# A two-layer attention kernel in a rebuilt form: weights split a unit ahead, norm and shared keys and values merged into the output of layer 0, plain f32 in layer 1's attention

## The reference, cut to what matters

```python
# layer 0: differential attention, 8 heads of two sub-heads of 64, causal with ALiBi
u = rms_norm(h, g) * (1 + scale) + shift
q, k, v, z = split(u @ w_in)                 # q and k normed per 64
o = (softmax(q1 k1) - lam * softmax(q2 k2)) @ v
h = h + gate * ((rms_norm(o, g2) * 0.8 * silu(z)) @ w_out)
# shared keys and values, made once from h
ks, vs = split((rms_norm(h, gkv) * (1 + s) + t) @ w_kv)   # ks normed; 2 heads of 64
# layer 1: 16 heads of 64 in two groups, window of 128 keys, a learned sink per head
u = rms_norm(h, gb) * (1 + scale) + shift
q, z = split(u @ w_in)                       # q normed per 64
o = softmax_with_sink(q ks) @ vs             # each 128 queries see 256 keys
h = h + gate * ((o * silu(z)) @ w_out)
```

## Time and profile before

| | us |
|---|---|
| median of 3 runs | 1358.45 |
| profiled execution | 1358.09 |
| its span | 1356.3 |
| busy PE / PEld / DVE / ACT / POOL | 1174.1 / 928.2 / 856.5 / 700.0 / 232.9 |
| mean granted clock of PE, of full speed | 0.967 |

### The profile page before, as it was taken

The page is one execution under the profiler, slowest core; times in us unless marked ns, Lnnn a source line. Parts: engine busy times, 40 slices in busy tenths (PEclk is TensorE's granted clock), DMA queues, the critical chain, the costliest instruction groups (busy, mean ns, idle before and its releaser), DMA issues.

```text
span 1356.3 us, 22457 instructions
## 1 busy us (share of the span) xinstructions
PE 1174.1 (87%) x6192; PEld 928.2 (68%) x6192; DVE 856.5 (63%) x2676; ACT 700.0 (52%) x2161; POOL 232.9 (17%) x354
## 2 busy tenths in 40 slices
PE   0469899998989899998975997679999898985998
PEld 0457576676757676675754885568888787875886
DVE  6665766666676766667664324976887888776221
ACT  0655555555555556555554104966776776674100
POOL 1201212112121211212101221111211212110122
PEclk9989999999999999999997998879999999997999
DMA  8342131312222131222214334110020100113332
GB/s 296 118 139 65 50 101 42 111 55 87 71 72 85 57 101 42 89 71 69 86 39 144 122 126 171 63 63 5 13 75 17 58 31 24 62 32 112 116 122 85
DMA packets 53226, 111.42 MB, mean 82 GB/s; under 512 B 5904, under 2 KB 19216, under 8 KB 52112
## 3 DMA queue, kind: packets, MB, share of 16 engines
q1 hardware_dynamic: 53136, 110.51, 24.8%
HBM read 93.71 MB, written 16.78 MB: 81 GB/s over the span
## 4 chain that ended last, share of the span: by engine, by line
PE 69%; DVE 12%; issue 8%; ACT 6%; DMA 3%; POOL 1%; DVEq 1%; POOLq 0%; ACTq 0%; SPq 0%
PE ps_p L591 12%; PE ps_p L593 11%; PE ps_p L592 11%; PE ps_s L671 5%; PE ps_o L706 3%; PE ps_t L731 3%; PE ps_p L815 2%; PE ps_p L816 2%; PE ps_p L817 2%; PE ps_o L817 2%; PE ps_o L815 2%; PE ps_o L816 2%; PE ps_t L792 2%; ACT e L952 2%; PE ps_s L744 2%
## 5 line engine op out<-in xcount | busy, mean ns | idle before, releaser
L591 PE MATMUL ps_p<-w_hi,u_hi 128*128 128x512 f32 x768 | 332.8, 433 | 13.0 <-DVE w_lo L1165 12.5
L593 PE MATMUL ps_p<-w_hi,u_lo 128*128 128x512 f32 x768 | 303.9, 396 | 0.0
L592 PE MATMUL ps_p<-w_lo,u_hi 128*128 128x512 f32 x768 | 302.8, 394 | 0.0
L591 PEld LDWEIGHTS ps_p<-w_hi,u_hi 128*128 128x128 f32 x768 | 146.2, 190 | 73.5 <-ACT ez L983 23.7
L593 PEld LDWEIGHTS ps_p<-w_hi,u_lo 128*128 128x128 f32 x768 | 145.4, 189 | 33.4
L592 PEld LDWEIGHTS ps_p<-w_lo,u_hi 128*128 128x128 f32 x768 | 146.9, 191 | 18.3
L952 ACT ACTIVATE e<-e,negm 128x256 f32<-128x256 f32 (+7 forms) x128 | 98.3, 769 | 113.4 <-DVE negm L1301 112.7
L1323 DVE TENSOR_REDUCE ssum<-sq 128x4 f32<-128x256 f32 x64 | 26.8, 419 | 122.2 <-ACT sq L978 122.2
L1018 ACT ACTIVATE pT<-ps_t 128x512 f32<-128x512 f32 (+2 forms) x96 | 44.6, 490 | 103.8 <-PE ps_t L731 103.3
L671 PE MATMUL ps_s<-kTa,qTa 64*128 64x512 f32 (+3 forms) x384 | 89.1, 541 | 8.3 <-DVE negm L1301 5.3
L1125 ACT ACTIVATE kT<-ps_t 128x512 fp32r<-128x512 f32 x32 | 17.4, 595 | 152.8 <-PE ps_t L828 152.8
(11 more groups left out here) (185 smaller groups left out, 2603.5 us busy)
## 6 DMA issues: line engine op xcount, KB each, us to landing
adabuf<-ada_w SPq DMA_DIRECT2D x64, 384.0 KB, 3.2
raw<-w_a SPq DMA_DIRECT2D x80, 256.0 KB, 3.4
raw<-w_b SPq DMA_DIRECT2D x48, 256.0 KB, 3.2
e<-ada_w SPq DMA_DIRECT2D x4, 1024.0 KB, 4.8
stage<-ada_w SPq DMA_DIRECT2D x4, 1024.0 KB, 4.9
e<-x SPq DMA_DIRECT2D x8, 512.0 KB, 3.4
oa_scratch<-ob SPq DMA_DIRECT2D x64, 64.0 KB, 1.6
e<-oa_scratch SPq DMA_DIRECT2D x8, 512.0 KB, 4.7
```

The costliest lines, as they stand in the source:

```text
L591: pe.matmul(o, u_hi[:, c, t], w_hi[:, c, :], start=(c == 0), stop=False)
L592: pe.matmul(o, u_hi[:, c, t], w_lo[:, c, :], start=False, stop=False)
L593: mm = pe.matmul(o, u_lo[:, c, t], w_hi[:, c, :], start=False, stop=(c == KD - 1))
```

## The change

The kernel is written anew with the same arithmetic for the large products.

- Weights: `w_hi` and `w_lo` have two buffers each, `raw` has four chunks instead of eight. One chunk of the next unit is loaded, split on ACT and split on DVE in each slot; GpSimd splits only the very first unit. The output matrix goes through the same buffers. Slots are written out for two units per turn of the loop (`unit_pairs`).
- Layer 0's slot on PE: scores, chunks 0 to 2, second scores, value product, query/key transposes, chunks 3 to 7, probability transposes. On ACT the split of a weight chunk stands ahead of the copy of the probabilities.
- Layer 1 has the same slot, one shorter than before. Scores, value products and transposes are plain f32: 4 matmuls of 64 x 256 (two row halves of the array), 8 of 128 x 64, 2 + 8 transposes. The final product is two DVE products of 256 columns, the first out of PSUM, and the gain of the queries is folded into the keys.
- Output: `oT` is one buffer of high and low, handled in halves; the accumulators are `ps_p` alone; SP has one residual buffer. For layer 0 the norm of tile s-2, the shared keys and values of tile s-3 (8 f32 matmuls of 256 columns) and the key transposes of tile s-4 stand in the same steps, with h taken from the chip's memory instead of being read back, and the first two projections of layer 1 follow inside.

The core of the diff (comment lines name the place):

```diff
 # PE, both layers: end of a slot (layer 0 shown)
-                    part_of_projection(range(3, 4))
                     if live(2):
                         pe.wait_ge(S.qn, n2 + 1)
                         if live(5):
                             pe.wait_ge(S.fin, n5 + 1)
                         for k in range(2):
                             mm = pe.transpose(ps_o[:, (i2 + 1) % 2, (2 + k) * P:(3 + k) * P], qn[:, k * P:(k + 1) * P], ident[:, :])
                         mm.then_inc(S.tr, 1)
-                    part_of_projection(range(4, 7))
+                    part_of_projection(range(3, KD))
                     if live(3):
...
                                 mm = pe.transpose(ps_t[:, j * P:(j + 1) * P], e0[:, i3 % 2, j * P:(j + 1) * P], ident[:, :])
                             mm.then_inc(S.pt, 1)
-                    part_of_projection(range(7, KD))
 # SP, loads of the weights and the output
+            def load_chunk(unit, c, src):
+                at_least(sp, w_lo_done, 8 * unit + c - RAW + 1)
+                sp.dma_start(raw[:, c % RAW, :], src).then_inc(w_loaded[c], 16)
...
+            def out_io(S, units, res_src, o_dram, dst, n0, with_next):
+                for s in range(NT + 1):
+                    n1 = s - 1
+                    if s < NT:
+                        m = n0 + s
+                        if s >= 2:
+                            sp.wait_ge(c_tr, 2 * (m - 1))
+                            sp.wait_ge(S.st[s % 2], 16 * ((units - 1) * NT // 2 + s // 2 + 1))
+                            sp.dma_start(e0[:, s % 2, :], o_dram[s * P:(s + 1) * P, :]).then_inc(c_o[s % 2], 16)
...
+                        at_least(sp, c_sum, m)
...
+                        sp.dma_start(flat(stage[:, 0:2, :]), res_src[s * P:(s + 1) * P, :]).then_inc(c_res, 16)
...
+                    if n1 >= 0:
+                        sp.wait_ge(c_sum, n0 + n1 + 1)
+                        sp.dma_start(dst[n1 * P:(n1 + 1) * P, :],
+                                     adabuf[:, (n1 % 2) * D:(n1 % 2 + 1) * D]).then_inc(c_st[n1 % 2], 16)
+                    if with_next and s in (2, 3, 4, 5):
+                        load_chunk(U_B, s - 2, w_b[0, :, s - 2, :])
 # PE, the output
+                for s in range(NT + (4 if with_next else 1)):
+                    n1, n2, n3, n4 = s - 1, s - 2, s - 3, s - 4
+                    if 0 <= n1 < NT:
+                        half(n1, 0)
+                    if s < NT:
+                        m = n0 + s
+                        pe.wait_ge(c_o[s % 2], 16 * (m // 2 + 1))
+                        at_least(pe, c_lo, 2 * m)
...
+                    if with_next and 0 <= n3 < NT:
...
+                        for c in range(KD):
+                            mm = pe.matmul(ps_o[:, n3 % 2, 0:256], stage[:, 2 + c // 4, (c % 4) * P:(c % 4 + 1) * P], wkv[:, c, :],
+                                           start=(c == 0), stop=(c == KD - 1))
+                        mm.then_inc(k_mm, 1)
+                    if with_next and 0 <= n2 < NT:
+                        pe.wait_ge(m_norm, n2 + 1)
...
+                    if 0 <= n1 < NT:
+                        half(n1, 1)
+                    if with_next and s in (NT + 1, NT + 2):
+                        project(b, False, 0, 0, s - NT - 1, s - NT - 1, range(KD))
 # DVE, the output
+                for s in range(NT + (4 if with_next else 1)):
...
+                    if with_next and 0 <= n2 < NT:
+                        product(n2, 1)
...
+                    if 0 <= n1 < NT:
+                        product(n1, 0)
+                        if not with_next:
+                            product(n1, 1)
...
+                    if s < NT:
+                        m = n0 + s
+                        for g in range(2):
+                            dve.wait_ge(c_hi, 2 * m + g + 1)
...
+                                dve.tensor_tensor(oT[:, 1, t], ps_t[:, t], oT[:, 0, t].bitcast(F32),
+                                                  ALU.subtract).then_inc(c_lo, 1)
...
+                    if with_next and s == NT:
+                        for c in range(KD):
+                            split_lo(U_B, c, 0)
 # ACT, the output: oT of the next tile is written when the second half has passed its fourth chunk
+                            act.wait_ge(c_tr, 2 * m + g + 1)
+                            if s:
+                                act.wait_ge(*((c_free, m) if g == 0 else (c_mm, 2 * m)))
 # DVE, layer 1: norm of the queries, then the final product of an old tile
+                        newton(slice(0, 4), S.y0, s - 1, S.step, 2 * (s - 2), S.rs)
+                        dve.wait_ge(S.rs, s - 1)
+                        head_norm(S, s, i2)
+                    if live(5):
+                        dve.wait_ge(S.pv, n5 + 1)
...
+                        dve.tensor_tensor(o, groups(ps_o[:, i5 % 2, 0:256], HD),
+                                          rl[:, i5 % 4, :].unsqueeze(2).to_broadcast([P, 4, HD]), ALU.mult).then_inc(b_half, 1)
+                        dve.wait_ge(b_half, n5 + 1)
+                        dve.wait_ge(S.zg, n5 + 1)
+                        dve.tensor_tensor(ob[:, i5 % 2, :], ob[:, i5 % 2, :], zs[:, i5 % 4, :], ALU.mult).then_inc(S.fin, 1)
 # ACT and DVE, one chunk of the next unit in a slot
+                elif i:
+                    split_hi(u + unit0 + 1, i - 1, 1 - par)
+                elif not (isinstance(u, int) and u == 0):
+                    split_hi(u + unit0, KD - 1, par)
```

More of the change, by code:

```diff
@@ L47 @@
 ADAW = 768
+RAW = 4
 C_VEC = 0
@@ L80, in stand_alone, with unit_pairs, flat, groups @@
     eng.sem_inc(passed, 1)
[L83 to L104, removed]
+def unit_pairs(eng, units, lags, slot):
+    for i in range(16):
+        slot(i // 8, i % 8, i // 8, lambda lag, i=i: i >= lag)
+    with eng.Fori(1, units // 2) as blk:
+        for i in range(16):
+            slot(2 * blk + i // 8, i % 8, i // 8, lambda lag: True)
+    for i in range(lags):
+        slot(units, i, 0, lambda lag, i=i: i < lag)
+def flat(t):
+    return t.rearrange("p a n -> p (a n)")
+def groups(t, c):
+    return t.rearrange("p (g c) -> p g c", c=c)
+def build(nc, x, par, rows_in, ada0_w, ada1_w, w_a, w_kv, w_b, out):
     h1 = nc.dram_tensor("h1_scratch", [SEQ, D], F32).ap()
@@ L119, in build @@
         u_lo = sb("u_lo", [P, KD, SEQ], F32R)
[L120 to L137, removed]
+        w_hi = [sb(f"w_hi{k}", [P, KD, FW], F32R) for k in range(2)]
+        w_lo = [sb(f"w_lo{k}", [P, KD, FW], F32R) for k in range(2)]
+        oT = sb("oT", [P, 2, D], F32R)
+        raw = sb("raw", [P, RAW, FW])
+        kT = sb("kT", [P, 2, SEQ])
+        qT = sb("qT", [P, 2, 256])
+        va = sb("va", [P, NT, P])
+        pT = sb("pT", [P, 1024])
         e0 = sb("e0", [P, 2, 1024])
@@ L194, in build @@
         ada0_mm = sem("ada0_mm")
+        ada_loaded = [sem(f"ada_loaded{k}") for k in range(2)]
+        ada_acc_done = sem("ada_acc_done")
+        ada_mm = sem("ada_mm")
         s_mod = sem("s_mod")
@@ L561, in _, with project @@
         def _(pe):
-            def adaln_first():
-                pe.wait_ge(s_const, 4)
-                pe.wait_ge(ada0_used, KD)
-                for j in range(ADA0 // P):
-                    mm = pe.matmul(ps_p[:, 0, j:j + 1], adabuf[:, j * P:(j + 1) * P], ones[:, :], start=True, stop=True)
-                mm.then_inc(ada0_mm, 1)
-            def project(S, is_a, u, it, n, chunks):
+            def project(S, is_a, u, par, it, n, chunks):
                 o = ps_p[:, it % 2, :]
-                if not len(chunks):
-                    return
+                first = isinstance(u, int) and u == 0
@@ new lines, in _ @@
+            pe.wait_ge(s_ident, 2)
+            pe.wait_ge(s_const, 4)
+            pe.wait_ge(ada0_used, KD)
+            for j in range(ADA0 // P):
+                mm = pe.matmul(ps_p[:, 0, j:j + 1], adabuf[:, j * P:(j + 1) * P], ones[:, :], start=True, stop=True)
+            mm.then_inc(ada0_mm, 1)
+            for s in range(NT + 1):
+                if s >= 1:
+                    n = s - 1
+                    dst = (ps_t, ps_s)[n % 2]
+                    pe.wait_ge(n_norm, n + 1)
+                    at_least(pe, n_umod_d, n - 1)
+                    at_least(pe, n_umod_a, n - 1)
+                    for d in range(KD):
+                        mm = pe.transpose(dst[:, d * P:(d + 1) * P], e0[:, n % 2, d * P:(d + 1) * P], ident[:, :])
+                    mm.then_inc(n_tr, 1)
+                if s in (6, 7):
+                    project(a, True, 0, 0, s - 6, s - 6, range(KD))
@@ L1019, in slot, with attn_b @@
                         last.then_inc(S.phi, 1)
[L1020 to L1028 removed]
+                unit_pairs(act, units, 5, slot)
+            def attn_b(S, units):
                 def exps(part, it, n):
```

1348 lines of the change are left out of this document (540 added, 808 removed).

## The result

The changed kernel takes 1408.8 us (median of four runs, 1406.5 to 1412.2) against 1358.0 before: a ratio of 1.0375, 95% interval 1.0355 to 1.0395. It is slower, as forecast, but by 51 us, not 13, and it lies above the stated range. Its profiled execution has a span of 1407.5 us against 1356.3.

What follows compares the result with a forecast made beforehand. PE was taken as the bound, busy nearly always in heads and outputs. Start +1, layer 0 heads -30, handover -8, merged output +5, layer 1 heads +24, last output +21: +13 on 1358.1, 1371 us, range 1330 to 1402.

Steps and rivals of the forecast that it cites:

- layer 1 (+24): Layer 1's heads: query transposes wait for DVE's product, slots of 10.85 us, stage 369 against 344.5 us: +24 us.
- 638.85 - 38: Layer 0 with handover: heads -30 us, handover to the output -8 us.
- 180 up to layer 1's first projection, and 140.6 against 123.5: Both outputs, rows' loads late: merged 180 against 175 us before (+5); last 123.5 against 102.3 (+21).
- The landing of the rows, 4.7 us: Both outputs: the load of a tile's rows lands 4.7 us after issue, at E + 10.3 merged, E + 9.1 last.
- The clock: Merged output: half clock for one gap a tile costs 1.7 us, six times, 10 us.
- Rival (C): Both outputs: clock halves once more in six merged tiles, once in six last ones, 20 us: 1391; chance 0.14.
- The start, +1: Start (95.5 us): GpSimd splits eight chunks instead of four, beside a chain that waits anyway: +1 us.
- the 1.7 us for restarts: Layer 0's unit start: restarts and short stops around the 4.2 us of waits, 1.7 of 5.9 us a unit gained.
- 3.8 - 1.9: Layer 0's new order, a unit: new waits cost 3.8 us (2.5 and 1.3), fewer projection cuts save 1.9.
- (A): Layer 1: query transposes do not wait, 32 slots at 9.7 us, -36: 1335; chance 0.15.
- (B): Output loads come in time, a queue reaching the waiting point earlier: -22, -25 and -10: 1314; chance 0.10.
- (D): Whole kernel: all new waits are hidden and PE's own work sets the end: 1290; chance 0.05.

Runs made afterwards that it cites:

- Runs 4 and 5: Changed kernel, layer 1 alone: query transposes two projection chunks later, 1371.6 us; or probability transposes one chunk before the slot's end, 1388.1 us.
- run 11: Changed kernel with twenty unused matmuls ahead of PE's wait for the rows in tiles 2 to 7 of the merged output: 1396.3 us.
- Run 12: Changed kernel, both outputs: rows' load still waits for the sum but is issued ahead of residual, store and weight chunk: 1358.3 us.
- run 2: Changed kernel, last output alone: DVE splits the next tile's rows ahead of the second gate product: 1423.3 us.
- Run 8: Changed kernel, start alone: loads of weight chunks 4 to 7 stand behind x loads, ACT splits them one a tile: 1405.1 us.
- run 6: Changed kernel, layer 0 alone in PE's order of before, weights still split a unit ahead: 1401.9 us.
- run 1: Changed kernel, both outputs: rows' load issued one step earlier, as soon as its buffer is free, not waiting for an older tile's sum: 1338.5 us.
- run 7: Changed kernel with twelve unused matmuls ahead of PE's wait for the rows in tiles 2 to 7 of the last output: 1403.3 us.
- after: The profiled run of the changed kernel with no further edit; that kernel's median time is 1408.8 us.

## Why the prediction was wrong

**What held.** The sign, which stages gain and which lose, and each new wait. The order of the losses did not: layer 1 (+24) was to lose most, and the last output did (+38). Layer 1: the stage from its first projection (897.3) takes 369.6 us, forecast 369; the wait is 1.19 us a slot, forecast 1.1; the slot 10.79, forecast 10.85. With T for the start of a slot (1068.13 in the lines above), PE reaches the transposes at T + 5.2 and goes on at T + 6.2, forecast 5.2 and 6.4. Runs 4 and 5 show the mechanism from both its ends. The f32 key/value matmuls, put at 3.5 us without a row of their own, take 3.46 at full clock (run 11). Layer 0 with handover: 602.9 us, forecast 638.85 - 38 = 600.9, but in part by luck, as below.

**What failed.** Of the 38 us between forecast and time 30 lie in the two outputs (193 us against 180 up to layer 1's first projection, and 140.6 against 123.5), where the waits were foreseen and their sizes were not. The steps that failed are two terms of the tile's sum: the landing of the rows and the clock behind the wait.

- **The landing of the rows, 4.7 us.** The step took it from the earlier trace rows, where the rows are issued right behind the store and ahead of the residual. Here they are the third 512 KB transfer of a burst (in four tiles of the merged output a weight chunk goes ahead of them too) and took 5.8 to 5.9 us. That is 1.1 us a tile in the last output. In the merged one the load landed at E + 11.6 to 12.2, forecast 10.3: 1.2 of landing, and 0.5 for the weight chunk's issue in those four tiles. Together some 16 us over twelve tiles. Run 12 shows it: first in the burst, the same load takes 3.9 us.
- **The clock.** The step allowed 1.7 us, a price that no row showed, in each of six merged tiles and nothing in the last output. The runs with PE kept busy give 2.1 us a merged tile and 5 to 10 us in all for the last output. Together about 10 us more; some 4 of the 30 us stay without a place. Rival (C) was this mechanism, put at 1391 with a chance of 0.14; its condition, a gap of over 4 us in a merged tile, came true (5.0 to 6.6 us), because of the landing. Its price did not: it had 2 x 1.7 = 3.4 us a merged tile where run 11 gives 2.1, and even so it lay 18 us below the time, as it left out the landing. With the landing alone the last output's tile is 15.45 + 1.1 = 16.55, and it took 16.9 where the clock stayed up; with both it is 18.15, and it took 18.0 to 19.2. The two errors are tied in the kernel: what makes the wait longer can also make what follows it slower, as run 2 shows with waits of 5.6 us and more.
- **The start, +1.** It was +5.9. I priced GpSimd's eight splits by what they do beside a waiting chain, and not by who queues behind the loads that wait for them: SP's list has the x loads there. Run 8 gives 3.4 of the 5.0 us at the first projection. For the rest, that GpSimd's splits slow DVE is only argued, and some of the +5.9 is scatter (the same start took 2 us less in run 6).
- **Layer 0, right by luck.** The unit fell from 77.9 to 74.1 us as forecast (73.9). But run 6 splits it: all that is new except PE's order brings 77.9 - 73.7 = 4.2 us, where the forecast had 5.9. That is as much as the waits of the earlier trace rows alone. It is a net figure, since run 6 still has waits of its own (7.1 us in 11 on the probabilities, 6.1 us in 4 on the maxima), so no run shows what the 1.7 us for restarts is by itself. And the new order costs 0.4 us a unit, not 3.8 - 1.9 = 1.9. The errors of 1.7 and 1.5 cancelled.

**The rivals.** (A), (B) and (D) rested on waits that hide; none did. (B) had SP's queue reach the waiting point sooner. A sooner queue was not needed for most of what it hoped for: the same transfers in another order (run 12) give 50 of the 70 us that run 1 gives.

**The rule on the clock.** Behind the waits of 2.7 to 3.2 us in the last output PE's clock fell in four of six tiles (1.23 to 1.97 us for eight transposes, against 1.09 in run 7). The Trainium skill, TensorE: Matmul & The Clock Gate, section "HAM oscillation", says that each burst behind a DMA wait of its loop starts cold again; the trace agrees for the merged tiles (1.97 us in all six, behind 5.0 to 6.6 us) and for four tiles of the last output, but the waits of 2.74 and 2.92 us there, shorter than those of the section's loop, were not followed by it. For the landing, the Trainium skill, DMA: Bandwidth & Descriptors, section "Queues, rings and completion order", says that each DMA engine takes a queue's descriptors in the order of its ring, and also that transfers need not complete in the order of issue; in run 12 and in after they landed in the order of issue.

**What stays open.** Why the old order of layer 0 saves 0.4 us a unit in spite of two more cuts a slot, which the forecast had put at 1.9 us a unit. Its waits on the probabilities grow (4.1 to 7.1 us) and those on the finished product (6.6 us) vanish; all of PE's listed waits in layer 0 fall from 19.1 us in after to 13.2 in run 6, which covers the 4.5 us gained and leaves next to nothing for the cuts.

## What to carry to other kernels

Where several transfers are issued together and one of them is waited for, issue that one first: here the order alone of three or four issues was worth 50 us, and the landing time of a transfer must be read from a burst like the one that it will be in. Price a wait of PE (TensorE) with the half-clock work that can stand behind it, and ask first what sets the step: an edit that removed a real stop of 1.5 us a tile cost 14 us while a load set the step, and brought 12 afterwards. A step moved earlier in an engine's strict order can meet a wait that it did not have before; in layer 1 two chunks of distance between it and that wait were worth 37 us.

## What the runs showed of the hardware

Three 512 KB transfers issued within a microsecond land after 3.9, 5.2 and 6.1 us, in the order of issue; the residual's load takes 4.2 us where it is issued first and 5.2 where it is second. Waits of PE of 2.7 to 3.2 us were followed by half clock in four tiles of six: 1.5 to 2.7 us a tile when they were. The clock fell behind a wait of 2.70 us and stayed up behind one of 2.92, so the length of the wait alone does not decide it here. And twelve matmuls a tile whose result nobody uses, put into such a wait, made the kernel 5.5 us faster.
